# Second FFN's third unit of a hybrid decoder layer: loaded chunks to other ring slots, activation sums split ahead of the first gate

## The reference, cut to what matters

```
def swiglu(h, w_in, w_out):
    g, u = jnp.split(h @ w_in, 2, axis=-1)
    return (jax.nn.silu(g) * u) @ w_out

x = layer_norm(DEEPNORM_ALPHA * x + g2 * (mixed @ w_o), ln_g[1], ln_b[1])
h = x * (1.0 + sc3) + sh3
x = layer_norm(DEEPNORM_ALPHA * x + FFN_RES * g3 * swiglu(h, f2_in, f2_out), ln_g[2], ln_b[2])
```

## Time and profile before

| | |
|---|---|
| median of three runs | 1485.7 us (1483.24 to 1486.34) |
| the profiled execution's own time | 1485.0 us |
| its span, first to last instruction | 1483.1 us |
| PE busy | 1397.5 us, 94% |
| DVE busy | 954.8 us, 64% |
| ACT busy | 593.9 us, 40% |
| POOL busy | 246.2 us, 17% |
| bytes moved | 257.75 MB, mean 174 GB/s |
| granted TensorE clock, mean | 0.988 |

### The profile page before, as it was taken

The page is one execution under the profiler, slowest core; times in us unless marked ns, Lnnn a source line. Parts: engine busy times, 40 slices in busy tenths (PEclk is TensorE's granted clock), DMA queues, the critical chain, the costliest instruction groups (busy, mean ns, idle before and its releaser), DMA issues.

```text
span 1483.1 us, 28611 instructions
## 1 busy us (share of the span) xinstructions
PE 1397.5 (94%) x10795; PEld 1174.6 (79%) x10795; DVE 954.8 (64%) x1782; ACT 593.9 (40%) x1172; POOL 246.2 (17%) x269
## 2 busy tenths in 40 slices
PE   4999999999999999998999999999989999999987
PEld 4788888899988878875666665567879988899976
DVE  2222373589957474545666666667889974899846
ACT  4322442144443322234555554564544431354510
POOL 1000220164500000010111010000045400455100
PEclk8999999999999999999999999999999999999998
DMA  9997263233332324248999998884132324232431
GB/s 312 371 379 259 73 186 108 61 89 93 108 113 79 108 66 149 85 152 314 333 338 341 347 345 303 301 298 148 29 92 86 108 79 135 86 94 86 128 107 64
DMA packets 182877, 257.75 MB, mean 174 GB/s; under 512 B 11403, under 2 KB 103313, under 8 KB 182746
## 3 DMA queue, kind: packets, MB, share of 16 engines
q1 hardware_dynamic: 182746, 255.97, 51.5%
HBM read 248.05 MB, written 7.88 MB: 173 GB/s over the span
## 4 chain that ended last, share of the span: by engine, by line
PE 59%; issue 21%; DVE 8%; DMA 4%; ACT 4%; SPq 2%; POOL 1%; ACTq 0%; DVEq 0%; POOLq 0%
PE ps L1179 19%; PE ps L571 15%; PE ps L329 6%; PE ps L2172 4%; PE ps L2237 3%; DVE ring_lo L1171 3%; PE ps L2184 2%; PE ps L575 2%; DMA ring_raw<-in_ffn_w_in_dram 2%; PE ps L1551 2%; PE ps L2218 2%; DMA wada<-in_w_ada_dram 1%; PE ps L2257 1%; PE ps L2271 1%; PE ps L313 1%
## 5 line engine op out<-in xcount | busy, mean ns | idle before, releaser
L1171 DVE TENSOR_TENSOR ring_lo<-ring_raw,ring_hi 128x512 fp32r<-128x512 f32 x293 | 267.2, 944 | 68.9 <-ACT ring_hi L1159 61.2
L1159 ACT ACTIVATE ring_hi<-ring_raw 128x512 fp32r<-128x512 f32 x326 | 188.2, 620 | 175.2 <-DMA ring_raw<-in_ffn_w_out_dram 85.9
L571 PE MATMUL ps<-ring_hi,f 128*128 128x512 f32 x704 | 218.4, 392 | 3.7 <-DVE ring_lo L1171 3.7
L1179 PE MATMUL ps<-hhi,ring_hi 128*128 128x288 f32 x588 | 174.7, 297 | 7.6 <-DVE ring_lo L1171 4.7
L1179 PE MATMUL ps<-hlo,ring_hi 128*128 128x288 f32 x588 | 173.2, 295 | 0.0
L571 PEld LDWEIGHTS ps<-ring_hi,f 128*128 128x128 f32 x704 | 132.4, 189 | 31.4 <-DVE ring_lo L1171 4.2
L571 PE MATMUL ps<-ring_lo,f 128*128 128x512 f32 x352 | 137.5, 391 | 0.0
L2172 PEld LDWEIGHTS ps<-ident,k_ring 128*128 128x128 f32 x832 | 92.2, 142 | 54.2 <-issue 34.9
L1179 PE MATMUL ps<-hhi,ring_lo 128*128 128x288 f32 x456 | 134.4, 295 | 0.0
L2172 PE MATMUL ps<-ident,k_ring 128*128 128x128 f32 x832 | 120.5, 282 | 10.6 <-DMA k_ring<-in_cache_diff_k_dram 5.2
L1179 PE MATMUL ps<-sumhi,ring_hi 128*128 128x288 f32 x396 | 119.1, 301 | 11.3 <-DVE ring_lo L1171 6.1
(11 more groups left out here) (297 smaller groups left out, 2917.0 us busy)
## 6 DMA issues: line engine op xcount, KB each, us to landing
wada<-in_w_ada_dram SPq DMA_DIRECT2D x18, 2048.0 KB, 14.4
ring_raw<-in_ffn_w_in_dram SPq DMA_DIRECT2D x140, 256.0 KB, 3.0
k_ring<-in_cache_diff_k_dram SPq DMA_DIRECT2D x128, 256.0 KB, 4.4
v_ring<-in_cache_diff_v_dram SPq DMA_DIRECT2D x124, 256.0 KB, 4.6
ring_raw<-in_ffn_w_out_dram SPq DMA_DIRECT2D x88, 256.0 KB, 3.3
k_ring<-in_cache_win_k_dram SPq DMA_DIRECT2D x16, 768.0 KB, 5.3
v_ring<-in_cache_win_v_dram SPq DMA_DIRECT2D x16, 768.0 KB, 7.1
w<-in_w_qkv_dram SPq DMA_DIRECT2D x21, 512.0 KB, 3.7
```

The source lines that it names most:

```text
L571: m = nc.tensor.matmul(ps[:, bank, :], x, w, start=(first and n == 0), stop=(last and n == 2), skip_group_check=True)
L1159: eng.activation(hi_of(g, i)[:], raw_of(g, i)[:], ACT.Copy).then_inc(sem("g_hi"), 1)
L1171: eng.tensor_tensor(lo_of(g, i)[:], raw_of(g, i)[:], hi_of(g, i)[:].bitcast(F32), ALU.subtract).then_inc(sem("g_lo"), 1)
L1179: m = nc.tensor.matmul(ps[:, bank, 0:TH], w, x, start=(first and n == 0), stop=(last and n == 2), skip_group_check=True)
```

## The change

Four edits, all about u2.

1. **Slots.** For u2 alone `slot_of` swaps A11 with S3, S1 with S2, and A22 with S4. So the chunks A11, S1 and A22 are loaded into slots 2, 1 and 5, which u0 never used, and the sums S3, S2 and S4 are written into slots 0, 3 and 6, which u0 gives back. `last_user` and the new `wait_slot` follow slots instead of operands, so the group after next (u4) waits for other operands of u2 than before.
2. **Loads.** u2's loads come in the order A11, S1, A22, A12, and all of the first three count on one semaphore; ahead of them SP waits until the last token tile has been evacuated. `ring_sums` has a wait on A12's landing ahead of S4 (in all groups).
3. **ACT.** High part of A11, three `sumhi`, and high parts of S2 and S3 now stand ahead of the gate of u0.
4. **DVE.** The three `sumlo` and the low parts of A11 and S2 stand ahead of the multiplication of u0, the low part of S3 ahead of u0's low part.

The diff, cut to its core:

```diff
@@ first_sums_vector
             if f == 1:
+                for i in (2, 3, 1):
+                    lower(i)
+                ring_lo_part(g, A11)
+                ring_lo_part(g, S2)
                 standard_mul(1, 0)
+                ring_lo_part(g, S3)
                 unit_lo(1, 0)
-                ring_lo_part(g, A11)
+                return
             lower(2)
             ring_lo_part(g, S2)
@@ slots
+        SWAPPED = {A11: S3, S3: A11, S1: S2, S2: S1, A22: S4, S4: A22}
+        def swapped(g):
+            return GROUPS[g] == (1, "in", FIRST[1])
+        def slot_of(g, i):
+            return SWAPPED.get(i, i) if swapped(g) else i
         def last_user(g, i):
-            return max((k for k in range(g - 2, -1, -2) if i in operands(k)), default=None)
+            return max(((k, j) for k in range(g - 2, -1, -2) for j in operands(k) if slot_of(k, j) == slot_of(g, i)), default=None)
+        def wait_slot(eng, g, i):
+            before = last_user(g, i)
+            if before is not None:
+                eng.wait_ge(sem("g_used"), count_before(*before) + 1)
         def loads_of(g):
+            if swapped(g):
+                return {A11: 0, S1: 0, A22: 0, A12: 1}
         def raw_of(g, i):
-            return first_raw if (g, i) == (0, S4) else ring_raw[g % 2][i]
+            return first_raw if (g, i) == (0, S4) else ring_raw[g % 2][slot_of(g, i)]
...
@@ ring_loads
+                if swapped(g):
+                    wait_evacuated(eng, MIX, PT_)
+                    wait_evacuated(eng, MIX + 1, PT_)
-                for i in operands(g) if kind == "out" else (A11, S1, A12, A22):
+                for i in operands(g) if kind == "out" else (A11, S1, A22, A12) if swapped(g) else (A11, S1, A12, A22):
                     before = last_user(g, i)
-                    if before is not None:
-                        if i == A22 and seven(before):
-                            eng.wait_ge(sem("g_lo"), count_before(before, A22) + 1)
-                        else:
-                            eng.wait_ge(sem("g_used"), count_before(before, i) + 1)
-                    dst = ring_raw[g % 2][i][:]
+                    if before is not None and before[1] == A22 and seven(before[0]):
+                        eng.wait_ge(sem("g_lo"), count_before(*before) + 1)
+                    else:
+                        wait_slot(eng, g, i)
+                    dst = raw_of(g, i)[:]
@@ ring_sums
             free(S4)
+            eng.wait_ge(landed_sem(g, A12), landed_by(g, A12))
@@ ffn_scalar
             else:
+                g = group_of(1, "in", FIRST[1])
+                ring_hi_part(g, A11)
+                first_sums_scalar(1)
+                ring_hi_part(g, S2)
+                ring_hi_part(g, S3)
                 eng.wait_ge(sem("g_used"), count_before(group_of(1, "in", 1)))
                 gate_both(1, 0)
-                first_sums_scalar(1)
                 unit_hi(1, 0)
-                for which in range(3):
-                    next_parts(ring_hi_part, group_of(1, "in", 1), which)
```

More of the change, by code:

```diff
@@ L1058, in raw_of @@
         def raw_of(g, i):
-            return first_raw if (g, i) == (0, S4) else ring_raw[g % 2][i]
+            return first_raw if (g, i) == (0, S4) else ring_raw[g % 2][slot_of(g, i)]
         def hi_of(g, i):
-            return first_hi if (g, i) == (0, S4) else ring_hi[g % 2][i]
+            return first_hi if (g, i) == (0, S4) else ring_hi[g % 2][slot_of(g, i)]
         def lo_of(g, i):
@@ L1066, in lo_of @@
                 return first_lo
-            return last_lo if i == A22 and seven(g) else ring_lo[g % 2][i]
+            return last_lo if i == A22 and seven(g) else ring_lo[g % 2][slot_of(g, i)]
         def ring_loads(f, w_in, w_out):
@@ L1128, in free @@
             def free(i):
-                before = last_user(g, i)
-                if before is not None:
-                    eng.wait_ge(sem("g_used"), count_before(before, i) + 1)
+                wait_slot(eng, g, i)
             eng.wait_ge(landed_sem(g, A11), landed_by(g, A11))
```

## The result

The changed kernel took 1476.27 us (median of 5 runs, 1474.89 to 1478.58); the kernel before, beside it, 1484.71 (5 runs). That is 8.4 us faster by the medians; the ratio is 0.9949, 95% interval [0.9936, 0.9963], which is a gain of 7.6 us (5.5 to 9.5). I had forecast 1480.0 within 1477.2 to 1483.2. So the direction was right and the gain was larger than the range allowed. The profiled executions were 1485.0 and 1478.58 us, their spans 1483.1 and 1476.7: 6.4 apart, not 8.4. Both numbers have to be explained.

What follows compares the result with a forecast made beforehand. PE bounds the kernel, busy 94%, with 7.78 us of waits at u2 and u3. Those and 0.9 of restarts go, against new waits of 0.6 + 1.8 + 0.7 + 0.2: 5.4 us gained, 1480 us, range 1477.2 to 1483.2.

Steps and rivals of the forecast that it cites:

- First wait, S2, S3: PE's waits at u2's first operand A11, S2 and S3, 1.70, 2.19 and 2.16 us, would all go.
- S1: At u2's S1 PE would start at 1093.8 instead of 1101.29; a wait of about 0.6 us stays.
- S4 and A22: Two new PE waits at u2, 1.8 and 0.7 us, with u4's first POOL sum ahead of u1's low part.
- a coin: At u4's first sum, its chunks' landing and DVE's readiness coincide at 1096.6; 0.2 us decides who goes first.
- Shift to the end: Behind u3 the old order is shifted as a whole; the gain carries to the end within 1 us.
- The added wait on A12's landing ahead of S4 costs nothing in other groups: In groups other than u2's, A12 and A22 count on one semaphore already waited for, so zero cost.
- No clock is to be won back: At PE's u2 waits the granted clock is 1.00, so no gain from the clock was counted.
- The table load: On ACT ahead of u0's gate: costs 1.28 us and no more, without the skill page's 1.38 us drain.
- A: Everything goes: u4's first sum lands behind u1's low part, turns cost PE nothing; gain 7.8 us, 1477.9; chance 0.12.
- B: Two more POOL turns ahead of steps b or c of u2 and u3; gain 3.1 us, 1482.6; chance 0.13.
- D: Slower: between u2's step c and u4's step b, eight POOL turns cost PE 9.2 us; 1489.5; chance 0.05.
- C: At u2 early loads do nothing, only the order of the splits counts; gain about 3 us, 1482.7; chance 0.08.

Runs made afterwards that it cites:

- slots alone: Swapped slots, early loads and early sums, with DVE's and ACT's order of splits as in the kernel before: 1480.47 us, 0.9966 to before.

## Why the prediction was wrong in size

*First wait, S2, S3.* Right: all three waits went. POOL's first sum started at 1077.56 (forecast 1077.5), the turns ran as counted, the low part of A11 was done ahead of PE, and the gate began at 1086.22 and ended at 1086.87 (forecast 1087.0).

*S1.* Right: 1093.86 with 0.48 us of wait, for 1093.8 and 0.6.

*S4 and A22: a term mis-sized.* The step that failed first was "POOL's first sum of u4 now takes its turn, 1.15 us, ahead of u1's low part", priced as waits of 1.8 and 0.7. Measured were 0.77 and 0.67. The sum started at 1097.38 and not at 1096.6, because it needs two chunks and I had both land after the 3.0 us of the earlier trace rows. By the trace of after they were issued at 1093.41 and 1093.83; the first landed at 1096.57, as forecast, the second at 1097.31, 3.5 us after its issue. I had seen that 0.2 us decide here and called it a coin. It fell on the same side in all seven profiles with u2 as after: the sum started 0.2 to 0.5 us behind the second instruction of u1's low part. I had named about 6.5 as the gain of the other side; it is what came, 6.2 us for 5.4. Where the turn is taken, with instructions added by hand, it cost PE 0.8 to 1.0 us of wait for the 1.15.

*Shift to the end.* Right in the profiled pair: 368.13 and 368.08 us behind the marker. That the two agree so closely is luck; single profiles differ there by up to 5.8 us with the clock.

*"The added wait on A12's landing ahead of S4 costs nothing in other groups".* Wrong as an argument. The semaphore had long been reached, and still the instruction behind it starts 0.07 us later, which turns a race that POOL won by 0.02 us. It moved PE's product by 1.1 us and took a clock fall away at 210 us. I looked for waits that it could add and not for an order that it could change.

*"No clock is to be won back".* True of the execution that I had, at 1.00. Of six profiles of kernels with u2 as before, the clock falls there in three. It costs time in two (markers 42.93 and 42.74, low for some 7 us) and none in the third (40.91, some 3 us); without a fall the marker is 40.86 to 41.08. In seven with u2 as after it never falls (34.58 to 34.85). The means are 41.6 and 34.8, so u2 is worth 6.8 us on average. The ratios of the changed kernel without the added wait agree: 0.9955 of 1485 twice, or 6.7 us, with intervals from 3.9 to 9.7 (5.5 and 8.0 by the medians).

*The rest of the sum.* 6.8 for u2 and 1.6 for the first FFN make 8.4, against gains of 8.4, 10.3 and 8.3 us by the medians and 7.6, 10.5 and 7.6 by the ratios. The 6.8 is shown by the profiles, and the timings agree. The 1.6 rests on the stretch in the profiles alone; the timings allow it and allow nothing as well. Beside this, the median of before was 1485.7 when I forecast and 1484.71 beside the result, which is 1.0 us of the 3.7 by which the forecast of 1480.0 was too long. So the forecast of the gain fell short by the turn at S4 (0.8), by the clock falls of before at u2 (0.6 on average), and by the first FFN (1.6, less sure).

*The table load.* Right as read from the earlier trace rows: gate 1.29 us behind the load's start again (1086.22 and 1084.93). The drain of the Trainium skill, "ScalarE: Activation LUTs", section "What ACT_TABLE_LOAD costs", doesn't show in this place either, and moving the load away changed nothing at PE.

*Rivals.* A had the order at u4's first sum right and its time (1477.9) was nearest, but waits at S1, S4 and A22 stayed, where A had none; its 7.8 us came close to the timed gain by luck. B and D did not occur; their mechanism exists, and with one or three POOL instructions added by hand the marker grew by 2.5 and 4.3 us. C was refuted by slots alone.

## What to carry to other kernels

Before pricing an edit at nothing because its semaphore is already reached, look for places where two engines that share turns start within 0.1 us of each other: a few hundredths reverse them. Where a wait of TensorE of 2 us or so is added or taken away, count a possible clock fall of up to 2 us with it, and take several profiles of the kernel before, since one profile may just miss it. Where the timed gain exceeds that of the stretch you changed, compare stretches of the whole program at fixed landmarks before inventing a cause.
